# A hybrid gMLP and differential-attention layer on eight cores: the schedule rebuilt around one x block and filled attention

## The reference

```
mod = silu(c) @ w_ada + b_ada ; shift, scale, gate = split(mod)
h   = rms_norm(x, norm_w) * (1 + scale) + shift
u_A, v_A, z_A, q_B, k_B, v_B, z_B = split(h @ w_in)        # 7 blocks of 512 columns
a = u_A * (tril(w_s) @ rms_norm(v_A) + b_s) * silu(z_A)    # chunks of 128 tokens, 4 groups
q, k = rope(rms_norm(q_B)), rope(rms_norm(k_B))            # 8 half heads of 64
o = (softmax(q1 k1') - lam * softmax(q2 k2')) @ v_B        # causal, 4 heads of 128
b = rms_norm(o, subln_w) * (1 - lam_init) * silu(z_B)
out = x + gate * (concat(a, b) @ w_out)
```

## Time and profile before

| | us |
|---|---|
| time, median of 3 runs (612.4 to 613.41) | 612.69 |
| the profiled execution | 611.3 |
| its span on the slowest core (core 2; cores 600.1 to 610.2) | 610.2 |
| TensorE matmul busy | 461.6 (76%) |
| VectorE busy | 341.9 (56%) |
| ScalarE busy | 312.1 (51%) |
| GpSimd busy | 33.6 (6%) |
| DMA | 50.64 MB, mean 83 GB/s |

### The profile page before, as it was taken

One profiled execution on the slowest core, in us unless ns is written; L12 is line 12 of the kernel. 1 busy time (PEld: TensorE's weight loads), 2 busy tenths in 40 slices (PEclk: granted clock), 3 DMA queues, 4 the chain that ended last, 5 costly groups with the idle time before them and its releaser, 6 DMA issues.

```text
span 610.2 us, 9622 instructions; the slowest of 8 cores (600.1 to 610.2 us)
## 1 busy us (share of the span) xinstructions
PE 461.6 (76%) x3204; PEld 233.9 (38%) x3232; DVE 341.9 (56%) x755; ACT 312.1 (51%) x416; POOL 33.6 (6%) x38
## 2 busy tenths in 40 slices
PE   0022249999999999999888789589669859939991
PEld 0000014444443433344443455456446536524440
DVE  2144595056717888854488354726645645664655
ACT  1132376566435767783122799669849939600000
POOL 2010000000000000000065200000000000000000
PEclk9975669999999999999799899869979969979997
DMA  8989970032704040050000620000000000044887
GB/s 235 258 263 244 346 147 2 10 61 104 168 5 70 2 65 5 1 105 0 2 1 2 128 46 3 1 2 1 2 1 3 2 1 2 2 138 138 246 263 249
DMA packets 21696, 50.64 MB, mean 83 GB/s; under 512 B 1424, under 2 KB 8848, under 8 KB 21648
## 3 DMA queue, kind: packets, MB, share of 16 engines
q1 hardware_dynamic: 12656, 39.22, 19.7%
q0 software_dynamic: 8992, 10.81, 11.6%
HBM read 51.40 MB, written 8.39 MB: 98 GB/s over the span
## 4 chain that ended last, share of the span: by engine, by line
PE 45%; DVE 15%; DMA 14%; ACT 12%; issue 10%; SPq 2%; DVEq 1%; ACTq 0%
PE psum L666 17%; PE psum L613 8%; ACT sb_regA L885 8%; PE psum L897 6%; DVE sb_regD L559 4%; DMA sb_szb<-xT 4%; PE psum L848 4%; DVE sb_regB L934 3%; DMA sb_regA<-xT 3%; DMA sb_regD<-x 3%; PE psum L974 2%; DMA out<-sb_regA 2%; SPq L94 2%; DMA out<-sb_regD 2%; PE psum L712 2%
## 5 line engine op out<-in xcount | busy, mean ns | idle before, releaser
L885 ACT ACTIVATE sb_regA<-psum,sb_small 128x1024 bf16<-128x1024 f32 x144 | 148.0, 1114 | 34.0 <-PE psum L848 24.9
L666 PE MATMUL psum<-sb_hT,sb_regC 128*128 128x512 bf16 x501 | 117.6, 384 | 6.0 <-ACT sb_hT L433 5.2
L897 PE MATMUL psum<-sb_vB,sb_regA 128*128 128x129 bf16 x1088 | 92.9, 230 | 3.7 <-DVE sb_regB L916 3.2
L613 PE MATMUL psum<-sb_regC,sb_hT 128*128 128x512 bf16 x375 | 87.3, 382 | 0.5
L848 PE MATMUL psum<-sb_qT,sb_kT 64*128 64x256 bf16 (+1 forms) x576 | 57.9, 278 | 35.7 <-DVE sb_hT L870 20.2
L897 PEld LDWEIGHTS psum<-sb_vB,sb_regA 128*128 128x128 bf16 x1088 | 67.8, 102 | 30.4 <-issue 29.9
L666 PEld LDWEIGHTS psum<-sb_hT,sb_regC 128*128 128x128 bf16 x512 | 50.3, 98 | 64.3 <-issue 9.3
L409 PE MATMUL psum<-sb_vB,sb_constb 128*128 128x512 bf16 x32 | 14.0, 618 | 69.2 <-ACT sb_vB L405 69.2
L613 PEld LDWEIGHTS psum<-sb_regC,sb_hT 128*128 128x128 bf16 x384 | 37.2, 99 | 45.1 <-issue 5.9
L848 PEld LDWEIGHTS psum<-sb_qT,sb_kT 64*128 64x128 bf16 x576 | 19.5, 94 | 55.7 <-issue 50.5
L409 PEld LDWEIGHTS psum<-sb_vB,sb_constb 128*128 128x128 bf16 x32 | 4.1, 137 | 78.3 <-issue 78.3
(11 more groups left out here) (126 smaller groups left out, 520.7 us busy)
## 6 DMA issues: line engine op xcount, KB each, us to landing
sb_regD<-x SPq DMA_DIRECT2D x16, 512.0 KB, 5.5
sb_qT<-w_adaT SPq DMA_DIRECT2D x15, 512.0 KB, 10.5
sb_regC<-w_in POOLq DMA_DIRECT2D x7, 1024.0 KB, 10.6
sb_regD<-w_adaT SPq DMA_DIRECT2D x9, 512.0 KB, 12.8
out<-sb_regD SPq DMA_DIRECT2D x8, 512.0 KB, 3.7
out<-sb_regA SPq DMA_DIRECT2D x8, 512.0 KB, 3.6
sb_szb<-xT SPq DMA_DIRECT2D x1, 2048.0 KB, 22.3
sb_kT<-xT SPq DMA_DIRECT2D x1, 2048.0 KB, 22.9
```

Of the source, the lines that this page charges most:

```text
L613: P.op("pe", lambda E, kc=kc: E.matmul(PS(bank), lhsT=hT[:, kc, 128 * tt:128 * (tt + 1)], rhs=wslot[ws_][:, kc, :], start=(kc == 0), stop= ...
L666: P.op("pe", lambda E, kc=kc: E.matmul(PS(bank), lhsT=wslot[ws_][:, kc, 128 * c4:128 * (c4 + 1)], rhs=hT[:, kc, cols], start=(kc == 0), st ...
L885: P.op("act", lambda E: E.activation(out=et, in_=psum[:, X:X + 2, :], func=AF.Exp, bias=negM, scale=0.125), reads=[pb[X], pb[Y], b_small], ...
L897: P.op("pe", lambda E, u=u, j=j, c=c, i=i: E.matmul(psum[:, 2 * a + j, 256 * c:256 * c + 129], lhsT=et[:, c, QB * u + 128 * j:QB * u + 128 ...
```

## The change

The schedule is written anew, with the same arithmetic but for the places named here.

- Lead: x block 0 is loaded first, in four pieces with a `Buf` each, then the w_ada rows in the order shift 0, scale 0, shift 1, ... through four slots. The rope tables are formed first of all, and the positions are loaded on ScalarE's queue with the small constants. As soon as one shift and one scale are there, that channel slice of h (block 0) is formed, on ScalarE, and the four V_B tiles of block 0 each accumulate one more chunk in four banks. x blocks 1 to 3 are loaded after the w_ada rows, and each is prepared on ScalarE (squares) and VectorE (all of the rest) between units of four tiles of V_B and Z_B.
- Then Z_A (SiLU straight into uz), Q and K. The gate is broadcast within Z_A. Under K, w_out is loaded in float32 rows and multiplied by the gate on GpSimd, so the output needs no gate.
- U, V_A and the gMLP move into attention as filler tiles, and so do the transposes and the half output tiles (512 columns) of finished query blocks. A credit of 0.80 us a step pays for fillers, at most two a step. They use two PSUM banks; the accumulators of attention have one pair of banks, which is copied to SBUF at the end of each group. Normalisation is on VectorE and GpSimd, a few steps later. U is multiplied onto uz from PSUM. The order of the groups changes: blocks 4 and 3 run one after the other at the end.
- Output half tiles are one addition of x from PSUM and, with the second half, one store.

```diff
-    for j in range(5):
-        matvec_dma(j)
-    load_xT(0)
-    for qt in range(4):
-        P.dma("pool", posc_i[32 * qt:32 * (qt + 1), :], pos1[512 * qt:512 * (qt + 1)].partition_broadcast(32),
-              b_posc, writes=[b_posc])
+    P.dma("sp", c_bc, c_d.rearrange("a n -> (a n)").partition_broadcast(128), b_F[0], writes=b_c)
+    P.dma("act", small[:, 56:94], spack_d, b_small, writes=[b_small])
+    P.dma("pool", constb[:, :], cb_d, b_constb, writes=[b_constb])
+    for qt in range(4):
+        P.dma("act", posc[32 * qt:32 * (qt + 1), :], pos1[512 * qt:512 * (qt + 1)].partition_broadcast(32),
+              b_F[4], writes=[b_F[4]])
+    P.dma("act", cf[:, :], cf_d, b_cf, writes=[b_cf])
...
+    load_xT(0)
...
+    for j in ADA[0:4]:
+        load_ada(j, (0, 1, 2, 3))
+    load_w(0, G_VB)
...
+    act(lambda E: E.activation(out=c_bc, in_=c_bc, func=AF.Silu), reads=b_c, writes=b_c)
...
+    rope_tables()
...
+    phaseA(0)
...
+    for n in range(16):
...
+        matvec(ADA[n])
+        if n + 4 < 16:
+            load_ada(ADA[n + 4], (0, 1, 2, 3))
+        if n == 1:
+            for q in range(4):
+                phaseM(0, q)
+        if n % 2 == 1:
+            kc = n // 2
...
+            phaseB(0, kc, "act" if kc < 7 else "dve")
+            for tt in range(4):
+                vb_main(tt, tt, kc)
+    load_xT(1)
+    load_w(1, G_ZB, extra=[x_last[1]])
+    load_xT(2)
+    load_xT(3)
...
+    prep(1)
+    unit(G_VB, 1, 0)
+    unit(G_ZB, 0, 1)
+    prep(2)
+    unit(G_ZB, 1, 1)
+    unit(G_VB, 2, 0)
+    prep(3)
...
+    unit(G_ZB, 2, 1)
+    unit(G_VB, 3, 0)
...
+    unit(G_ZB, 3, 1)
...
+                P.dma("sp", stg[m % 2], wout_d[128 * m:128 * (m + 1), :], b_stg[m % 2], writes=[b_stg[m % 2]])
+                pool(lambda E, m=m: E.tensor_tensor(out=woutb[:, m, :], in0=stg[m % 2], in1=gate_bc, op=ALU.mult),
+                     reads=[b_stg[m % 2]] + b_vn[0:4], writes=[b_wo])
...
+        for j in range(2):
+            dve(lambda E, j=j: E.tensor_copy(out=raw[a][:, j, :, 0:129], in_=O4[:, j, :, 0:129]),
+                reads=[pb[j]], writes=[b_rw[a][j]])
...
+            def post():
+                a = n % 2
+                for h in range(4):
+                    dve(lambda E, h=h: E.scalar_tensor_tensor(
+                        out=gm[a][:, 128 * h:128 * (h + 1)], in0=PS(bank, 128 * h, 128 * (h + 1)),
+                        scalar=sguwT[:, h:h + 1], in1=bs_bc[:, 128 * h:128 * (h + 1)], op0=ALU.mult, op1=ALU.add),
+                        reads=[pb[bank], b_bs, b_small], writes=[b_gm[a]])
...
+        def post():
+            dve(lambda E: E.tensor_tensor(out=ost[s_][:, cc], in0=PS(bank), in1=xres[s_][:, cc], op=ALU.add),
+                reads=[pb[bank], b_xr[s_]], writes=[b_os[s_]])
+            if half == 1:
+                P.dma("sp", out_d[rows_, :], ost[s_], b_os[s_], reads=[b_os[s_]], writes=[b_out])
...
+    for tb in range(TB):
+        for c4 in range(4):
+            fillq.append(("u", u_tile(c4, tb), 1.73))
+        if tb >= 1:
+            for n in range(4 * tb - 4, 4 * tb):
+                fillq.append(("g", gmlp(n), 0.22, n))
+        for tt in range(4 * tb, 4 * tb + 4):
+            fillq.append(("v", va_tile(tt), 1.73))
+    for n in range(12, 16):
+        fillq.append(("g", gmlp(n), 0.22, n))
+
+    FB = [2, 3]
...
+    RATE = 0.80
...
     for gs in range(NS):
...
+        et, ei = do_exp(gs)
+        if gs + 2 < NS:
+            do_qk(gs + 2)
+        do_pv(gs, et, ei)
         if last:
...
+            group_end(gs, jq, h)
+        run_posts()
+        run_due(gs)
+        credit += RATE
+        k = 0
+        while k < 2:
+            i = next_fill()
+            if i is None or not (credit >= fillq[i][2] or (last and credit > -1.0 and k == 0)):
+                break
+            if fillq[i][0] == "out" and len(fillq) <= 3 and gs < NS - 2:
+                break
+            credit -= fill_one()
+            k += 1
```

More of the change, by code:

```diff
@@ L305, in _build_body, with FU_ @@
+    ost = [W[:, 2048 + 1024 * i:2048 + 1024 * (i + 1)] for i in range(2)]
+    def FU_(i, n=1):
+        return F[:, 512 * i:512 * (i + n)]
     B = {}
@@ new lines, in phaseA @@
+    def phaseA(tb):
+        r_ = tb % 2
+        bank = 6 + r_
+        sb_ = b_vn[8 * r_:8 * r_ + 8]
+        for q in range(4):
+            act(lambda E, q=q: E.activation(out=sqx[r_][:, 2 * q:2 * q + 2, :], in_=xs[tb][:, 2 * q:2 * q + 2, :], func=AF.Square),
+                reads=[b_xs[tb][q]], writes=sb_[2 * q:2 * q + 2])
+            for kc in (2 * q, 2 * q + 1):
+                pe(lambda E, kc=kc: E.matmul(PS(bank), lhsT=ones_b, rhs=sqx[r_][:, kc, :], start=(kc == 0), stop=(kc == KC - 1)),
+                   reads=[b_constb, sb_[kc]], writes=[pb[bank]])
+        act(lambda E: E.activation(out=rstd_t[tb], in_=PS(bank), func=AF.Ln, bias=epsn, scale=1.0 / D),
+            reads=[pb[bank], b_sc], writes=[b_rstd[tb]])
+        act(lambda E: E.activation(out=rstd_t[tb], in_=rstd_t[tb], func=AF.Exp, scale=-0.5),
+            reads=[b_rstd[tb]], writes=[b_rstd[tb]])
@@ new lines, in _build_body @@
+    unit(G_VB, 2, 0)
+    prep(3)
+    for j in range(16, 18):
+        load_ada(j, (2, 3))
+    load_w(2, G_ZA, extra=[x_last[3]])
+    late_loads()
+    unit(G_ZB, 2, 1)
+    unit(G_VB, 3, 0)
+    load_w(0, G_K, extra=[x_last[3]])
+    for j in range(16, 24):
+        matvec(j)
+        if j + 2 < 24:
+            load_ada(j + 2, (2, 3))
+    dve(lambda E: E.tensor_tensor(out=gate, in0=modraw[:, 16:24], in1=bada[:, 16:24], op=ALU.add),
+        reads=[b_small] + b_raw_[16:24], writes=[b_gate])
@@ L859, in do_qk, with do_exp @@
         state[gs] = sl
[L861 to L878 removed]
+    def do_exp(gs):
         sl = state.pop(gs)
@@ L884, in do_exp_pv @@
         et = e_tiles[ei].rearrange("p (a b) -> p a b", a=2)
[L885 to L893 removed]
+        act(lambda E: E.activation(out=et, in_=psum[:, X:X + 2, :], func=AF.Exp, bias=negM, scale=0.125),
+            reads=[pb[X], pb[Y], b_lam], writes=[b_e[ei]])
@@ new lines, in u_tile, with run @@
+    def u_tile(c4, tb):
+        def run(bank):
+            cols = slice(512 * tb, 512 * (tb + 1))
+            for kc in range(KC):
+                pe(lambda E, kc=kc: E.matmul(
+                    PS(bank), lhsT=wsl[1][:, kc, 128 * c4:128 * (c4 + 1)], rhs=hT[:, kc, cols],
+                    start=(kc == 0), stop=(kc == KC - 1)), reads=[b_h[tb][kc], b_w[1]], writes=[pb[bank]])
+            def post():
+                dve(lambda E: E.tensor_tensor(out=uz[:, c4, cols], in0=PS(bank), in1=uz[:, c4, cols], op=ALU.mult),
+                    reads=[pb[bank], b_uz[tb]], writes=[b_uz[tb]])
+            return post
+        return run
@@ new lines, in run_due, with next_fill @@
+    def run_due(s):
+        for it in [x for x in due if x[0] <= s]:
+            due.remove(it)
+            it[1]()
+    def next_fill():
+        for i, it in enumerate(fillq):
+            if it[0] == "g" and it[3] not in vn_done:
+                continue
+            if it[0] == "v" and not tm_free[va_ctr[0] % 2]:
+                continue
+            if it[0] == "out" and any(o[0] in ("u", "g", "v") for o in fillq[0:i]):
+                return None
+            return i
+        return None
@@ L942, in _build_body, with fill_one @@
+    def fill_one():
+        it = fillq.pop(next_fill())
+        kind, run, wt = it[0:3]
+        bank = FB[fb_ctr[0] % 2]
+        fb_ctr[0] += 1
+        posts.append(run(bank))
+        return wt
+    RATE = 0.80
+    credit = 0.0
     do_qk(0)
@@ L1001, in _build_body @@
+    s = NS
+    while due or fillq or posts:
+        now[0] = s
+        run_posts()
+        run_due(s)
+        for k in range(2):
+            if len(posts) < 2 and next_fill() is not None:
+                fill_one()
+        s += 1
     P.emit()
-    for bb in b_ost:
-        if bb.dsem is not None:
-            nc.sync.wait_ge(bb.dsem, bb.dcnt)
+    for bb in b_os:
+        nc.sync.wait_ge(bb.dsem, bb.dcnt)
 def _consts():
-    cst = np.zeros((128, CO_END), np.float32)
     p = np.arange(128)
-    cst[:, CO_IDENT:CO_IDENT + 128] = np.eye(128, dtype=np.float32)
```

1251 lines of the change are left out of this document (587 added, 664 removed).

## The result

| | us |
|---|---|
| time after, median of 4 runs (671.74 to 692.46) | 681.69 |
| time before, median of 4 runs | 613.05 |
| ratio | 1.100, 95% interval 1.087 to 1.114 |
| forecast | 558, range 522 to 594 |

The account below looks back on a forecast made before the run. Bounds: the lead, attention with no engine full, and an output stage waiting for transfers. Sum: 279.5 us before attention, 264.9 in it (544.4), then 5 and 6 of tail: span 555.4, forecast 558, range 522 to 594.

Parts of the forecast that it names:

- The lead: Start to V_B of block 0: a series from chained position loads through rope, unfolds and modulation products, ending at 80.5 us.
- The four x blocks: V_B and Z_B stage: x blocks 1 to 3 land late, 48 us of matmuls take 82, stage ends about 163.
- Blocks 2 and 3 repeat a pattern: V_B and Z_B: queued squares hold TensorE 3 us, and waiting for h costs 5 us more.
- The floor of attention: Attention steps without fillers: 0.79 us for 112 steps, 0.86 for 32 diagonal ones, 116 us in all.
- ScalarE and Pool have slack: Attention with fillers: TensorE is the bound at about 1.6 us a step, 234.4 us in all; the others have room.
- (a) to (c): Attention losses not hidden: fillers running out 7 us, PV waiting for raw copies 3.5, gMLP clusters on VectorE 20.
- the tail: After attention: last normalisation 5 us, then an add and a store, 6 us.
- Term (c): gMLP in attention: two chunks a step put 5.2 us on VectorE; four clusters cost 20 us, 5 to 35 possible.
- no longer stand in a chain: Output stage: its 82 us shrinks to the tail because the x loads are unchained and the gate multiply is gone.
- Rival 3: Attention: recurring bank waits hold TensorE at 1.2 GHz for a third of 218 us, costing 73: 631 us; chance 0.07.
- The dense-load form of rival 3: Matmul-bound work: dense cores lower the clock to 13/16, 91 us more on 394, giving 649 us; chance 0.01.
- Folding the gate into w_out: Under K: Pool work of eight 128x1024 products, costed at nothing; uncovered it would be some 20 us.

Follow-up runs that it names:

- the mended kernel: Changed kernel plus unchained position loads, earlier x, later V_A and norm sums, spread gMLP, ScalarE sharing h, sub-layer weight off GpSimd, V_A overwrite fixed: 602.55 us, ratio 0.9858.
- the position edit: Changed kernel with a buffer object for each of the four position loads, so none waits for the one before: ratio 1.0777, 14 us less.

## Why the prediction was wrong

- **The lead** was right within 4 us. The last position load was issued at 20.6 (forecast 20), the unfolds took 9.57 (9.5), the squares 3.89 (3.6). One load was overlooked: the packed constants stand behind the positions in ScalarE's queue and land at 28.5, so the rope chain starts there and not at 25. V_B 0 ends at 84.4 (80.5), h of block 1 is complete at 100.4 (99).
- **The four x blocks** failed by 13 us, in the term "Blocks 2 and 3 repeat a pattern". It took block 1's durations; in blocks 2 and 3 GpSimd works beside VectorE and stretches its operations by up to 1.6 times in the mean. Without that product this stretch is 8 us shorter. The product on GpSimd was in the change and had no price in the sum. On some cores the load of Z_B's weights, 21.93 us beside the x blocks, cost 7 more; its landing wasn't asked for either.
- **The floor of attention** failed. "QK 0.32 and eight PV matmuls 0.46" took the best distance of each, but the PV matmuls of a step take 0.56 when scores follow: 0.88 and not 0.79. With a tile it is 2.60 and not 2.52. Over 144 steps that is an estimated 13 us.
- **"ScalarE and Pool have slack"** was the costly step. It reads busy shares; ScalarE was indeed busy for less than half of attention (172.67 of 370.5 us), but each engine works its queue in order, and what counted was what stood ahead of the exponentials there. The not-hidden terms (a) to (c) and the tail had 41.5 us of idle TensorE; there were 87.4. Term (c), the gMLP clusters, was there in kind (8.4 us of direct waits for the evacuation L984, and 8.7 for V_A's product L962), and spreading the gMLP took 12 us off. V_A's chain over four engines had no term at all; it cost 24 us, by the run that only moved it.
- **The x load.** The tail was costed as "an add and a store", and rows 1 had shown an output stage waiting for transfers. The loads of x were said to "no longer stand in a chain"; the wait for them was moved into attention. It cost 20 us.
- **The lowered clock.** The sum priced 234.4 us at 2.4 GHz. TensorE was busy 283.1: 234.4, 13 for the step's floor, and some 36 left for the lower clock (22 in the mended kernel). An estimate from the clock alone agrees: a mean of 0.88 between the two levels is about 89 of 370.5 us at 1.2 GHz; with TensorE busy for 0.76 of them half of 68 us is extra, 34. Rival 3 named this mechanism and gave it 0.07. Its price was 73 with waits taken as in the forecast; the real case was half of that, plus the waits themselves. Its sign, a clock below 0.9 in filled attention, came true (0.88). What spoke for it was in the earlier trace rows: attention stood at 0.91 before, where TensorE had waited 20.2 us for one copy of VectorE (L870), and the change gave the other engines more to do between TensorE's steps. A clock of 0.91 on 234.4 us would alone have been 23 us in the sum.
- **The dense-load form of rival 3** was dismissed too flatly with "show nothing of it". That holds for the kernel before, whose eight cores all stand at 1.00 from 182 to 262 us. But in the kernel of the position edit core 0 has this stretch of Z_A (columns as above):

```profile
168.00:175.00 7.00, 7.00 (x28) 2.90 (x27) 2.44 (x4) 1.79 (x3) 0.00 (x0) 0.81 0.85 182
```

  TensorE is busy all the time, at 0.81. Cores 1 to 3 have 0.81 there too, cores 4 to 7 0.91 to 0.94; from 190 us on core 0 is back at 1.00. In the changed kernel core 5 (first fence) and core 1, both in output tiles without a wait, differ in the same way:

```profile
541.26 1.22 PE L1015 MATMUL psum<-sb_WO,sb_uz 128*128 128x512 bf16 x4
542.31 1.23 PE L1015 MATMUL psum<-sb_WO,sb_qT 128*128 128x512 bf16 x4
```

```profile
542.74 1.03 PE L1015 MATMUL psum<-sb_WO,sb_uz 128*128 128x512 bf16 x4
543.61 1.03 PE L1015 MATMUL psum<-sb_WO,sb_qT 128*128 128x512 bf16 x4
```

  Four matmuls from start to start take 1.05 us on core 5 and 0.87 on core 1, 1.21 times; core 5's granted clock is 0.78 there (501 to 541). That is neither the 2.4 nor the 1.2 GHz level. The Trainium skill, TensorE: Matmul & The Clock Gate, Seeing it yourself, has a whole die at 13/16 of the clock once three of its cores run dense matmuls, which would be 1.23 times: the size agrees in both traces. The extent does not: cores 6 and 7, of core 5's die, stand at 0.96 and 0.91 from 501 to 541, and no core of the changed kernel is below 1.00 from 184 to 292 us, in Z_A, Q and K. On core 1 no part of the 108 us is of this form; where it comes it cost little (72 matmuls of Z_A in 18.4 us on core 1 of the position edit, and the next 72 in 15.7).
- **Folding the gate into w_out** at nothing was right: eight products on GpSimd of 2359 ns each lie under K, and TensorE is busy 112.2 of the 117.2 us there.

Of the 108 us on core 1: 13 came before attention, 46 are idle time above the forecast's, 49 are slower matmuls. In the mended kernel the idle time is 48.6 us, near the forecast's 41.5, and the matmuls 269.9. What stays open is how much of the lowered clock would go if the last waits went; no run here had TensorE free of them for all of attention.
